# Two blocks of a transformer on one core: the moving columns of every gemm pass read as i and i+128 in turns

## The chip, the cores and the metric

The kernel runs on one core of one Trainium2 chip (trn2). The metric is device time in microseconds (us) of one execution; the median of the runs is compared. TensorE, VectorE (DVE in the profile), ScalarE (ACT), GpSimd (POOL) and SyncE (SP, which here issues the weight loads) run side by side and meet at semaphores.

## The reference

Two transformer blocks over one sequence of 256 tokens with 2048 channels, everything in float32. Cut to what matters here, it is a long row of products of a 256-row activation with a weight matrix:

```python
def first_block(x, ...):
    h = x + _gla_mixer(_rmsnorm(x, gla_norm), ...)       # h @ w_in (q, k, v, r), gated linear attention, @ w_out
    h = h + _sq_relu_mlp(_rmsnorm(h, mlp_norm), w_up, w_down)
    return _rmsnorm(h, final_norm)

def _sq_relu_mlp(h, w_up, w_down):                        # 2048 -> 8192 -> 2048
    a = jax.nn.relu(h @ w_up)
    return (a * a) @ w_down

def second_block(x, ...):
    proj = rms_norm(x, norm_mix_g) @ w_in                 # q, k, v, conv and gate inputs, three branch gates
    y_a, y_b, y_c = ...                                   # attention, gated recurrence, short convolution
    x = x + (g_a * y_a + g_b * y_b + g_c * y_c) @ w_out
    x = x + jnp.square(jax.nn.relu(rms_norm(x, norm_mlp_g) @ w_mlp_up)) @ w_mlp_down
    return rms_norm(x, final_g)
```

## The kernel before

**Arithmetic of a product.** TensorE multiplies in the format fp32r, which holds fewer bits than float32. So each operand is split into a high part (a copy cast to fp32r) and a low part (what the copy lost), and a product is the sum of high x high, high x low and low x high. Activations lie transposed in SBUF, channels on partitions: `xs`, `hs`, `mixs` and `ycs` are `[128, k-tile, 2, 256]`, where the 2 is high and low and the 256 are tokens. Weights are loaded in units of 4 k-tiles x 256 columns (512 KB) into one of four slots of `raw`; ScalarE writes the high part (L820) and VectorE the low part (L1142) into `wsp`.

**A pass.** `gemm` (L509) produces one block of 256 output channels by 256 tokens. It goes over its units (usually four, 16 k-tiles), and for each k-tile over the two halves `j` of 128 output channels. For each it issues a pair of matmuls into the PSUM tile `acc[:, g, j]`, two rows of 256 columns: L530 takes the high weights as stationary operand and streams 512 moving columns, the 256 high tokens and the 256 low tokens, so that row 0 gets high x high and row 1 high x low; L532 takes the low weights, streams the 256 high tokens and adds into row 1. Where the result is wanted with tokens on partitions (the blocks "gv" and "v", `tokens_out`), the roles change: L525 and L527 take a tile of the activation as stationary operand and stream the weights, which `both_parts` views as `[128, 2, 256]`. In all cases the moving columns are read in the order in which they lie, 256 neighbours and then 256 others.

```python
pe.matmul(acc[:, g, j], w_part(0, slot)[:, t, cols], x[:, k0 + k], start=start,
          stop=False, skip_group_check=True)
ins = pe.matmul(acc[:, g, j, 1], w_part(1, slot)[:, t, cols], x[:, k0 + k, 0],
                start=False, stop=stop, skip_group_check=True)
```

**After a pass.** `g` alternates, so the sums of one pass are read while the next runs; a pass begins when the sums of the pass two before it have been read (`main_read`). ScalarE copies row 1 of both halves into `corr` (`evac`, L831); VectorE adds row 0 and `corr` into `z` (`take`, L1152, and the same line in `first_take` for the first block). From `z` the rest follows: scaling, squared relu, residual, split into high and low for the next product. The last block of the kernel has a tail of its own, `finish` (L1394 on VectorE, L1009 on ScalarE), with the additions split by half (L1399, L1401, L1402, L1405).

**Order of the work.** Each engine has its program written out by hand; the same walk over the blocks (`straight_walk`, `mlp_walk`, `mix_walk`) is used on all of them. ScalarE and VectorE split the weights of the next block while TensorE runs this one. The attention, gating, recurrence and norm matmuls (L612, L643, L658, L761 and others) are plain fp32 or fp32r matmuls between passes, and a short extra matmul (`spacer`, L507) stands in some passes.

Of the kernel before, what the change touches and what calls it, by code (L numbers as in the profile page):

```python
# [16 lines left out]
ALU = mybir.AluOpType  # L17
# [3 lines left out]
P = 128  # L21
# [96 lines left out]
def build(nc, a, out, scratch):  # L118
# [3 lines left out]
    def at(name, shape, dt=F32, offset=None):  # L122
        size = -(-int(np.prod(shape[1:])) * 4 // 32) * 32
        if offset is None:
            offset = top[0]
            top[0] += size
        return nc.alloc_sbuf_tensor_at(name, shape, dt, offset=offset)
# [6 lines left out]
    def w_part(k, slot):  # L134

        n = UK * NB
        start = HIGHS + k * LOWS + slot * n
        return wsp[:, start:start + n].rearrange("p (t n) -> p t n", t=UK)

    def both_parts(slot, t):  # L140

        row = (slot * UK + t) * NB
        return wsp[:, HIGHS:HIGHS + 2 * LOWS].rearrange("p (k n) -> p k n", k=2)[:, :, row:row + NB]
# [41 lines left out]
    corr = at("corr", [P, 2, 2, T])  # L185
    z = at("z", [P, 2, T])
# [32 lines left out]
    def psum(name, shape):  # L219
        return ctx.enter_context(nc.psum_tensor(name, shape, F32))  # L220

    acc = psum("acc", [P, 2, 2, 2, T])
# [3 lines left out]
    def sem(name):  # L226
        return ctx.enter_context(nc.semaphore(name))
# [3 lines left out]
    corr_ready, main_read = sem("corr_ready"), sem("main_read")  # L231
# [32 lines left out]
    end_corr, end_main, end_sum, end_sq = sem("end_corr"), sem("end_main"), sem("end_sum"), sem("end_sq")  # L264
# [4 lines left out]
    def prm(name, j=0, n=1):  # L269
        r = ROWS[name][0] + j  # L270
        return par[:, bass.ds(r, n)] if not isinstance(r, int) else par[:, r:r + n]

    def bc(ap, n=2):

        return ap[:].unsqueeze(1).to_broadcast([P, n, T])

    def kt_of(t, k):

        return t[:, k] if isinstance(k, int) else t[:, bass.ds(k, 1)].squeeze(1)
# [53 lines left out]
    def units_of(round_, first, n):  # L333

        return [(round_ + (first + k) // SLOTS, (first + k) % SLOTS) for k in range(n)]
# [162 lines left out]
    def _(pe):  # L498
# [6 lines left out]
        def spacer(to):  # L505

            pe.matmul(to[:, 0:SPACE], xs[:, 0, 0, 0:P], xs[:, 0, 0, 0:SPACE], start=True, stop=True, skip_group_check=True)  # L507

        def gemm(b, units, g, x, ready, k0=0, tokens_out=False, mid=None, before=None, mid_unit=2, spaced=False):  # L509

            if not (isinstance(b, int) and b < 2):
                pe.wait_ge(main_read, b - 1)
            for u, (rnd, slot) in enumerate(units):
                if before:
                    before(u)
                pe.wait_ge(lo_done, SLOTS * rnd + slot + 1)
                for s, v in ready(u):
                    pe.wait_ge(s, v)
                for t in range(UK):
                    k = UK * u + t  # L520
                    start, stop = k == 0, (u == len(units) - 1 and t == UK - 1)
                    for j in range(2):
                        cols = slice(j * P, j * P + P)
                        if tokens_out:
                            pe.matmul(acc[:, g, j], x[:, k0 + k, 0, cols], both_parts(slot, t), start=start,  # L525
                                      stop=False, skip_group_check=True)
                            ins = pe.matmul(acc[:, g, j, 1], x[:, k0 + k, 1, cols], w_part(0, slot)[:, t],  # L527
                                            start=False, stop=stop, skip_group_check=True)
                        else:
                            pe.matmul(acc[:, g, j], w_part(0, slot)[:, t, cols], x[:, k0 + k], start=start,  # L530
                                      stop=False, skip_group_check=True)
                            ins = pe.matmul(acc[:, g, j, 1], w_part(1, slot)[:, t, cols], x[:, k0 + k, 0],  # L532
                                            start=False, stop=stop, skip_group_check=True)
                        if spaced is True and u == t == j == 0:
                            spacer(acc[:, g, 1, 0])
                        if spaced == "late" and u == 0 and (t, j) == (UK - 1, 0):
                            spacer(flat[1])
                        if mid and u == mid_unit + 1 and (t, j) == (UK - 1, 0):
                            spacer(flat[1])
                ins.then_inc(unit_used, 1)  # L540
                if mid and u == mid_unit:
                    mid()
# [243 lines left out]
        for k in range(3):  # L786
            if k:
                pe.wait_ge(end_sq, k)
            for j in range(TT):
                part = sq[:, 0, k - 1, j * P:(j + 1) * P] if k else ssq[:, 0, j * P:(j + 1) * P]  # L790
                ins = pe.matmul(flat[2 * j][:, 0:2], part, ones[:, 0:2], start=(k == 0), stop=(k == 2),
                                skip_group_check=True)
# [5 lines left out]
    def look_ahead(rnd, first, n):  # L798

        return units_of(rnd + 1, first, n)  # L800
# [6 lines left out]
    def _(act):  # L807
# [32 lines left out]
        def squares(n, i, gain=None):  # L840

            if not (n == 1 and isinstance(i, int) and i == 0):
                act.wait_ge(ssq_done, 8 * (n - 1) + i)
            ins = act.activation(sq[:, 0], pair(xres, i), ACT.Square)  # L844
            if gain:
                for j in range(2):
                    ins = act.activation(sq[:, 1, j], kt_of(xres, 2 * i + j), ACT.Square, scale=prm(gain, 2 * i + j))
            ins.then_inc(sq_ready, 1)
# [281 lines left out]
    def _(dve):  # L1130
        own = Steps(dve, dve_steps)
# [6 lines left out]
        def split_lo(rnd, slot):  # L1138
            if is_past_end(rnd):
                return  # L1140
            dve.wait_ge(hi_done, SLOTS * rnd + slot + 1)
            dve.tensor_tensor(w_part(1, slot), raw[:, slot], w_part(0, slot).bitcast(F32),  # L1142
                              ALU.subtract).then_inc(lo_done, 1)

        def take(b, rnd, first, n, g, then=None):

            for r, s in look_ahead(rnd, first, n)[:-1]:
                split_lo(r, s)
            if then:
                then()  # L1150
            dve.wait_ge(corr_ready, b + 1)
            dve.tensor_tensor(z[:], acc[:, g, :, 0], corr[:, g], ALU.add).then_inc(main_read, 1)  # L1152
            dve.wait_ge(main_read, b + 1)

        def last_split(rnd, first, n):
# [8 lines left out]
        def gained(i, gain):  # L1164

            for j in range(2):
                g = gmix[:, bass.ds(2 * i + j, 1)] if gain == "gmix" else prm(gain, 2 * i + j)
                ins = dve.tensor_scalar(h[:, j], kt_of(xres, 2 * i + j), g, None, ALU.mult)
            ins.then_inc(value_ready, 1)
# [9 lines left out]
        for i in range(PAIRS):  # L1179
            dve.wait_ge(hi_ready, i + 1)  # L1180
            for j in range(2):
                ins = dve.scalar_tensor_tensor(out=xs[:, 2 * i + j, 1], in0=M[i % 4][:, j], scalar=prm("gla_norm", 2 * i + j),
                                               in1=xs[:, 2 * i + j, 0].bitcast(F32), op0=ALU.mult, op1=ALU.subtract)
# [6 lines left out]
        def first_take(g):  # L1190

            for u in range(4):
                split_lo(1, u)
            dve.wait_ge(std_done, 1)
            own.done(dve.reciprocal(rcol[:], rcol[:]))
            dve.wait_ge(const_done, 1)
            for j in range(TT):
                ins = dve.tensor_scalar(h[:, 0, j * P:(j + 1) * P], ident[:], rcol[:, j:j + 1], None, ALU.mult)
            ins.then_inc(diag_ready, 1)
            dve.wait_ge(corr_ready, 1)  # L1200
            dve.tensor_tensor(z[:], acc[:, g, :, 0], corr[:, g], ALU.add).then_inc(main_read, 1)
            dve.wait_ge(main_read, 1)

        def first_keys():
# [189 lines left out]
        def finish(rnd, g, gain):  # L1394

            r, s = units_of(rnd, 0, 4)[-1]
            x = [kt_of(xres, 2 * (PAIRS - 1) + j) for j in range(2)]
            dve.wait_ge(unit_used, SLOTS * r + s + 1)
            dve.tensor_tensor(x[1], x[1], acc[:, g, 1, 0], ALU.add).then_inc(end_main, 1)  # L1399
            dve.wait_ge(end_corr, 1)  # L1400
            own.done(dve.tensor_tensor(x[0], x[0], acc[:, g, 0, 0], ALU.add))  # L1401
            dve.tensor_tensor(x[0], x[0], corr[:, g, 0], ALU.add).then_inc(end_sum, 1)  # L1402
            dve.wait_ge(end_main, 1)
            dve.wait_ge(end_corr, 2)
            dve.tensor_tensor(x[1], x[1], corr[:, g, 1], ALU.add).then_inc(end_sum, 1)  # L1405
            dve.wait_ge(end_sum, 2)
            dve.wait_ge(y_mm, PAIRS - 1)
            gained(PAIRS - 1, gain)
# [199 lines left out]
```

## Time and profile before

| | |
|---|---|
| runs (us) | 2659.05, 2659.95, 2656.82; median 2659.05 |
| profiled execution, span from first to last instruction | 2658.5 us; no separate time of this execution is given |
| TensorE matmul busy | 2642.8 us, 99% |
| weight loads into TensorE busy | 2336.9 us, 88% |
| VectorE, ScalarE, GpSimd busy | 1787.8 (67%), 1350.7 (51%), 96.3 us (4%) |
| chain that ended last | TensorE 94%, DMA 3%, VectorE 2%, ScalarE 1% |
| DMA | 504.65 MB, mean 190 GB/s |
| mean granted TensorE clock | 0.998 |

How to read it: a row of the profile names a line of the kernel, the engine, the operation, out<-in by the names of the tiles, shapes and a count. Matmuls are pipelined and each row's duration includes the way through the array, so the durations of neighbours overlap; the distance from one start to the next is what a matmul occupies. "Idle before" is the time that an engine stood still just before a group, with what ended it. The clock is given as a share of full speed, 2.4 GHz; the other level is 1.2 GHz.

### The profile page before, as it was taken

The page shows a single profiled execution, that of the slowest core. Times are in us where ns is not written, and L with a number is a line of the kernel's source. Part 1 is how long each engine was busy: PE and PEld are TensorE (multiplying, and loading weights), DVE is VectorE, ACT ScalarE, POOL GpSimd, SP SyncE. Part 2 cuts the span into 40 slices and gives each one's busy share as a digit, 9 for nine tenths or more (in the row PEclk, how much of TensorE's full clock was granted, in tenths as well). Part 3 has the DMA queues.
Part 4 walks back from the last instruction along what each step waited for, and adds up shares of the span by engine and source line. Part 5 has one row for each costly group of instructions (what it writes and reads, how often), then busy time and mean ns, then how long its engine had stood idle before and what let it go on. Part 6 is the DMA issues. An engine that isn't in the chain of part 4 may idle for free.

```text
span 2658.5 us, 43594 instructions
## 1 busy us (share of the span) xinstructions
PE 2642.8 (99%) x15628; PEld 2336.9 (88%) x15628; DVE 1787.8 (67%) x2067; ACT 1350.7 (51%) x1635; POOL 96.3 (4%) x96
## 2 busy tenths in 40 slices
PE   9999999999999999999999999999999999999998
PEld 8888888888888888888888888888888888888887
DVE  6667777666566567866887666666776566665665
ACT  6546555444444445544675555555554444444444
POOL 1000020000000002200000000000110000000001
PEclk9999999999999999999999999999999999999999
DMA  7794666666666666665556655566666666666664
GB/s 223 167 212 129 205 192 194 192 190 193 194 190 197 194 192 189 211 208 167 159 180 192 198 190 189 189 193 202 196 191 191 190 192 196 190 196 196 191 194 138
DMA packets 507428, 504.65 MB, mean 190 GB/s; under 512 B 17908, under 2 KB 505609, under 8 KB 507337
## 3 DMA queue, kind: packets, MB, share of 16 engines
q1 hardware_dynamic: 506060, 501.79, 60.5%
q10 hardware_dynamic: 1276, 1.63, 1.5%
q8 instruction: 59, 0.97, 0.2%
q14 instruction: 33, 0.26, 0.0%
HBM read 499.69 MB, written 3.67 MB: 189 GB/s over the span
## 4 chain that ended last, share of the span: by engine, by line
PE 94%; DMA 3%; DVE 2%; ACT 1%; issue 0%; SPq 0%; DVEq 0%; ACTq 0%
PE acc L530 60%; PE acc L532 30%; DMA raw<-in_gla_w_in 3%; PE acc L525 1%; DVE wsp L1142 1%; PE acc L527 1%; ACT wsp L820 0%; DVE lat L1474 0%; DMA xtok<-in_x 0%; PE misc L643 0%; PE misc L658 0%; PE misc L761 0%; PE misc L612 0%; PE misc L660 0%; PE misc L581 0%
## 5 line engine op out<-in xcount | busy, mean ns | idle before, releaser
L1142 DVE TENSOR_TENSOR wsp<-raw,wsp 128x1024 fp32r<-128x1024 f32 x944 | 1166.6, 1242 | 577.4 <-ACT wsp L820 547.1
L530 PE MATMUL acc<-xs,wsp 128*128 128x512 f32 x4224 | 1446.8, 390 | 1.1 <-issue 0.4
L820 ACT ACTIVATE wsp<-raw 128x1024 fp32r<-128x1024 f32 x944 | 993.4, 1057 | 688.1 <-PE acc L532 602.0
L532 PE MATMUL acc<-xs,wsp 128*128 128x256 f32 x4224 | 1166.5, 276 | 0.0
L530 PEld LDWEIGHTS acc<-xs,wsp 128*128 128x128 f32 x4224 | 793.4, 188 | 166.3 <-DVE wsp L1142 1.8
L530 PE MATMUL acc<-hs,wsp 128*128 128x512 f32 x2560 | 873.0, 389 | 0.0
L532 PEld LDWEIGHTS acc<-xs,wsp 128*128 128x128 f32 x4224 | 793.4, 188 | 0.5
L532 PE MATMUL acc<-hs,wsp 128*128 128x256 f32 x2560 | 706.6, 276 | 0.0
L530 PEld LDWEIGHTS acc<-hs,wsp 128*128 128x128 f32 x2560 | 480.6, 188 | 99.4
L532 PEld LDWEIGHTS acc<-hs,wsp 128*128 128x128 f32 x2560 | 480.6, 188 | 0.0
L831 ACT ACTIVATE corr<-acc 128x512 f32<-128x512 f32 x246 | 146.9, 597 | 370.1 <-PE acc L532 360.1
L1152 DVE TENSOR_TENSOR z<-acc,corr 128x512 f32<-128x512 f32 x246 | 169.9, 691 | 215.3 <-ACT corr L831 215.2
L525 PE MATMUL acc<-wsp,xs 128*128 128x512 f32 x384 | 134.9, 395 | 1.7 <-issue 1.7
L471 POOL TENSOR_TENSOR ssq<-ssq,sq 128x256 f32<-128x256 f32 x37 | 30.4, 828 | 2495.7 <-ACT sq L844 1842.8
L527 PE MATMUL acc<-wsp,xs 128*128 128x256 f32 x384 | 107.1, 279 | 0.0
L525 PEld LDWEIGHTS acc<-wsp,xs 128*128 128x128 f32 x384 | 72.1, 188 | 19.7 <-issue 2.7
L530 PE MATMUL acc<-mixs,wsp 128*128 128x512 f32 x256 | 87.1, 389 | 0.0
L838 ACT ACTIVATE hs<-z 128x512 f32 (+1 forms) x64 | 40.5, 633 | 90.6 <-DVE z L1370 90.6
L527 PEld LDWEIGHTS acc<-wsp,xs 128*128 128x128 f32 x384 | 72.0, 188 | 0.0
L532 PE MATMUL acc<-mixs,wsp 128*128 128x256 f32 x256 | 70.7, 276 | 0.0
L1349 DVE TENSOR_TENSOR xres<-xres,z 128x512 f32 (+1 forms) x79 | 54.7, 693 | 12.1 <-DVE z L1152 11.8
L530 PEld LDWEIGHTS acc<-mixs,wsp 128*128 128x128 f32 x256 | 48.1, 188 | 9.8
(243 smaller groups left out, 1059.8 us busy)
## 6 DMA issues: line engine op xcount, KB each, us to landing
raw<-in_w_in SPq DMA_DIRECT2D x224, 512.0 KB, 4.4
raw<-in_mlp_w_up SPq DMA_DIRECT2D x128, 512.0 KB, 4.0
raw<-in_mlp_w_down SPq DMA_DIRECT2D x128, 512.0 KB, 4.4
raw<-in_w_mlp_up SPq DMA_DIRECT2D x128, 512.0 KB, 4.0
raw<-in_w_mlp_down SPq DMA_DIRECT2D x128, 512.0 KB, 4.2
raw<-in_gla_w_in SPq DMA_DIRECT2D x96, 512.0 KB, 4.9
raw<-in_gla_w_out SPq DMA_DIRECT2D x32, 512.0 KB, 4.2
raw<-in_w_out SPq DMA_DIRECT2D x32, 512.0 KB, 4.0
```

The costliest lines, as they stand in the source:

```text
L471: pool.tensor_tensor(ssq[:, k], ssq[:, k], sq[:, k, 0], ALU.add).then_inc(ssq_half, 1)
L525: pe.matmul(acc[:, g, j], x[:, k0 + k, 0, cols], both_parts(slot, t), start=start, stop=False, skip_group_check=True)
L527: ins = pe.matmul(acc[:, g, j, 1], x[:, k0 + k, 1, cols], w_part(0, slot)[:, t], start=False, stop=stop, skip_group_check=True)
L530: pe.matmul(acc[:, g, j], w_part(0, slot)[:, t, cols], x[:, k0 + k], start=start, stop=False, skip_group_check=True)
L532: ins = pe.matmul(acc[:, g, j, 1], w_part(1, slot)[:, t, cols], x[:, k0 + k, 0], start=False, stop=stop, skip_group_check=True)
L820: act.activation(w_part(0, slot), raw[:, slot], ACT.Copy).then_inc(hi_done, 1)
L831: act.activation(corr[:, g], acc[:, g, :, 1], ACT.Copy).then_inc(corr_ready, 1)
L838: act.activation(pair(dst, i)[:, :, 0], src[:], ACT.Copy).then_inc(hi_ready, 1)
L1142: dve.tensor_tensor(w_part(1, slot), raw[:, slot], w_part(0, slot).bitcast(F32), ALU.subtract).then_inc(lo_done, 1)
L1152: dve.tensor_tensor(z[:], acc[:, g, :, 0], corr[:, g], ALU.add).then_inc(main_read, 1)
L1349: own.done(dve.tensor_tensor(pair(xres, i), pair(xres, i), z[:], ALU.add))
```

## The change

All matmuls of `gemm` read their moving operand through a view, `taking_turns`, that takes column i and column i+128 of each 256 in turns: 0, 128, 1, 129, and so on. High and low parts stay apart, so a 512-column matmul reads the 256 high ones in this order and then the 256 low ones. They write the PSUM columns in the order in which they come, one next to the other, so that PSUM column 2i holds column i and 2i+1 holds i+128. ScalarE's copy to `corr` keeps that order. The additions that join the two sums read PSUM and `corr` through `in_order`, every second column and then the ones between, and write their result in natural order, seen as two halves (`halves`). The stationary operands, the matmuls outside `gemm`, the semaphores and the number of instructions of each engine stay as they are.

```diff
+    def taking_turns(ap):
+
+        dims = "p s (u i) -> p s i u" if len(ap.shape) == 3 else "p (u i) -> p i u"
+        return ap.rearrange(dims, u=2)
+
+    def in_order(ap):
+
+        dims = "p s (i u) -> p s u i" if len(ap.shape) == 3 else "p (i u) -> p u i"
+        return ap.rearrange(dims, u=2)
+
+    def halves(ap):
+
+        dims = "p s (u i) -> p s u i" if len(ap.shape) == 3 else "p (u i) -> p u i"
+        return ap.rearrange(dims, u=2)
...
                     for j in range(2):
-                        cols = slice(j * P, j * P + P)
+                        cols, both = slice(j * P, j * P + P), acc[:, g, j].rearrange("p a b -> p (a b)")
                         if tokens_out:
-                            pe.matmul(acc[:, g, j], x[:, k0 + k, 0, cols], both_parts(slot, t), start=start,
+                            pe.matmul(both, x[:, k0 + k, 0, cols], taking_turns(both_parts(slot, t)), start=start,
                                       stop=False, skip_group_check=True)
-                            ins = pe.matmul(acc[:, g, j, 1], x[:, k0 + k, 1, cols], w_part(0, slot)[:, t],
+                            ins = pe.matmul(acc[:, g, j, 1], x[:, k0 + k, 1, cols], taking_turns(w_part(0, slot)[:, t]),
                                             start=False, stop=stop, skip_group_check=True)
                         else:
-                            pe.matmul(acc[:, g, j], w_part(0, slot)[:, t, cols], x[:, k0 + k], start=start,
+                            pe.matmul(both, w_part(0, slot)[:, t, cols], taking_turns(x[:, k0 + k]), start=start,
                                       stop=False, skip_group_check=True)
-                            ins = pe.matmul(acc[:, g, j, 1], w_part(1, slot)[:, t, cols], x[:, k0 + k, 0],
+                            ins = pe.matmul(acc[:, g, j, 1], w_part(1, slot)[:, t, cols], taking_turns(x[:, k0 + k, 0]),
                                             start=False, stop=stop, skip_group_check=True)
...
-            dve.tensor_tensor(z[:], acc[:, g, :, 0], corr[:, g], ALU.add).then_inc(main_read, 1)
+            dve.tensor_tensor(halves(z[:]), in_order(acc[:, g, :, 0]), in_order(corr[:, g]), ALU.add).then_inc(main_read, 1)
...
+            x = [halves(xj) for xj in x]
-            dve.tensor_tensor(x[1], x[1], acc[:, g, 1, 0], ALU.add).then_inc(end_main, 1)
+            dve.tensor_tensor(x[1], x[1], in_order(acc[:, g, 1, 0]), ALU.add).then_inc(end_main, 1)
             dve.wait_ge(end_corr, 1)
-            own.done(dve.tensor_tensor(x[0], x[0], acc[:, g, 0, 0], ALU.add))
-            dve.tensor_tensor(x[0], x[0], corr[:, g, 0], ALU.add).then_inc(end_sum, 1)
+            own.done(dve.tensor_tensor(x[0], x[0], in_order(acc[:, g, 0, 0]), ALU.add))
+            dve.tensor_tensor(x[0], x[0], in_order(corr[:, g, 0]), ALU.add).then_inc(end_sum, 1)
             dve.wait_ge(end_main, 1)
             dve.wait_ge(end_corr, 2)
-            dve.tensor_tensor(x[1], x[1], corr[:, g, 1], ALU.add).then_inc(end_sum, 1)
+            dve.tensor_tensor(x[1], x[1], in_order(corr[:, g, 1]), ALU.add).then_inc(end_sum, 1)
```

## Rows read from the trace of the kernel before

**Rows 1.** The page: span, busy times and the granted clock in 40 slices.
```profile
span 2658.5 us, 43594 instructions
...
PE 2642.8 (99%) x15628; PEld 2336.9 (88%) x15628; DVE 1787.8 (67%) x2067; ACT 1350.7 (51%) x1635; POOL 96.3 (4%) x96
...
PEclk9999999999999999999999999999999999999999
```

**Rows 2.** The page: the chain that ended last, by engine and line.
```profile
PE 94%; DMA 3%; DVE 2%; ACT 1%; issue 0%; SPq 0%; DVEq 0%; ACTq 0%
PE acc L530 60%; PE acc L532 30%; DMA raw<-in_gla_w_in 3%; PE acc L525 1%; DVE wsp L1142 1%; PE acc L527 1%; ACT wsp L820 0%; DVE lat L1474 0%; DMA xtok<-in_x 0%; PE misc L643 0%; PE misc L658 0%; PE misc L761 0%; PE misc L612 0%; PE misc L660 0%; PE misc L581 0%
```

**Rows 3.** Groups by line: shapes, count, busy us, mean ns, idle before.
```profile
L530 PE MATMUL acc<-xs,wsp 128*128 128x512 f32 x4224 | 1446.8, 390 | 1.1 <-issue 0.4 <-DVE wsp L1142 0.4
...
L532 PE MATMUL acc<-xs,wsp 128*128 128x256 f32 x4224 | 1166.5, 276 | 0.0
...
L530 PE MATMUL acc<-hs,wsp 128*128 128x512 f32 x2560 | 873.0, 389 | 0.0
...
L525 PE MATMUL acc<-wsp,xs 128*128 128x512 f32 x384 | 134.9, 395 | 1.7 <-issue 1.7
...
L530 PE MATMUL acc<-mixs,wsp 128*128 128x512 f32 x256 | 87.1, 389 | 0.0
...
L530 PE MATMUL acc<-ycs,wsp 128*128 128x512 f32 x128 | 43.9, 389 | 0.0
```

**Rows 4.** Busy time by stretch, 500 us of the first MLP.
```profile
core 0: us, PE busy (x) PEld busy (x) DVE busy (x) ACT busy (x) POOL busy (x), PEclk, DMA share, GB/s
500.00:1000.00 500.00, 500.00 (x2943) 442.88 (x2942) 315.67 (x322) 229.46 (x253) 0.00 (x0) 1.00 0.62 193
```

**Rows 5.** TensorE in order of time (start us, us), in both MLPs.
```profile
600.00 0.39 PE L530 MATMUL acc<-xs,wsp 128*128 128x512 f32 x1
600.22 0.28 PE L532 MATMUL acc<-xs,wsp 128*128 128x256 f32 x1
600.34 0.39 PE L530 MATMUL acc<-xs,wsp 128*128 128x512 f32 x1
...
2640.07 0.39 PE L530 MATMUL acc<-hs,wsp 128*128 128x512 f32 x1
2640.30 0.28 PE L532 MATMUL acc<-hs,wsp 128*128 128x256 f32 x1
2640.41 0.39 PE L530 MATMUL acc<-hs,wsp 128*128 128x512 f32 x1
```

**Rows 6.** The same view in the two token-major stretches.
```profile
135.09 0.39 PE L525 MATMUL acc<-wsp,xs 128*128 128x512 f32 x1
135.32 0.28 PE L527 MATMUL acc<-wsp,xs 128*128 128x256 f32 x1
135.43 0.39 PE L525 MATMUL acc<-wsp,xs 128*128 128x512 f32 x1
...
1199.80 0.40 PE L525 MATMUL acc<-wsp,xs 128*128 128x512 f32 x1
1200.04 0.28 PE L527 MATMUL acc<-wsp,xs 128*128 128x256 f32 x1
1200.16 0.40 PE L525 MATMUL acc<-wsp,xs 128*128 128x512 f32 x1
```

**Rows 7.** Plain fp32 matmuls, 256 columns: order of time, and their group.
```profile
1290.46 1.03 PE L761 MATMUL misc<-lat,wax 128*128 128x256 f32 x4
...
L761 PE MATMUL misc<-lat,wax 128*128 128x256 f32 x32 | 8.2, 379 | 0.0
```

**Rows 8.** Groups by line on VectorE: far steps against neighbours.
```profile
L1283 DVE TENSOR_TENSOR btot<-btot,mn 128x8 f32<-128x8 f32 x3 | 0.5, 173 | 0.1
L1285 DVE TENSOR_TENSOR dec<-btot 128x8 f32<-128x8 f32 x6 | 0.6, 163 | 0.0
...
L1142 DVE TENSOR_TENSOR wsp<-raw,wsp 128x1024 fp32r<-128x1024 f32 x944 | 1166.6, 1242 | 577.4 <-ACT wsp L820 547.1 <-DVE hs L1160 17.0 <-DVE mixs L1160 0.4
L1349 DVE TENSOR_TENSOR xres<-xres,z 128x512 f32 (+1 forms) x79 | 54.7, 693 | 12.1 <-DVE z L1152 11.8
```

**Rows 9.** The joining additions: their group, and order of time at the end.
```profile
L1152 DVE TENSOR_TENSOR z<-acc,corr 128x512 f32<-128x512 f32 x246 | 169.9, 691 | 215.3 <-ACT corr L831 215.2
...
2647.83 0.42 DVE L1401 TENSOR_TENSOR xres<-xres,acc 128x256 f32<-128x256 f32 x1
...
2648.28 0.42 DVE L1402 TENSOR_TENSOR xres<-xres,corr 128x256 f32<-128x256 f32 x1
2648.63 0.42 DVE L1405 TENSOR_TENSOR xres<-xres,corr 128x256 f32<-128x256 f32 x1
```

**Rows 10.** Waits: who waited for whom, us in total, times, longest.
```profile
ACT wsp L820 <- PE acc L532: 602.0, 442, 1.7
DVE wsp L1142 <- ACT wsp L820: 547.1, 501, 6.2
ACT corr L831 <- PE acc L532: 360.1, 223, 2.2
DVE z L1152 <- ACT corr L831: 215.2, 220, 1.5
```

More of the change, by code:

```diff
@@ L1200, in first_take @@
             dve.wait_ge(corr_ready, 1)
-            dve.tensor_tensor(z[:], acc[:, g, :, 0], corr[:, g], ALU.add).then_inc(main_read, 1)
+            dve.tensor_tensor(halves(z[:]), in_order(acc[:, g, :, 0]), in_order(corr[:, g]), ALU.add).then_inc(main_read, 1)
             dve.wait_ge(main_read, 1)
```

## The prediction

> **What bounds the kernel now.** I read the page's busy shares first: TensorE works 99% of a span of 2658.5 us, and its granted clock is at the upper level in every slice [rows 1]. The chain that ended last gives TensorE 94%, of which 90% are the two matmuls of a gemm pass, L530 and L532 [rows 2]. Then the count: 4224 + 2560 + 256 + 128 = 7168 pairs of a 512-column and a 256-column matmul there, and 384 such pairs in the two token-major groups, L525 and L527, 7552 pairs in all [rows 3]. Busy time says little about matmuls that overlap, so I take the distance between starts. In the MLP stage 2943 matmuls fill 500 us, 0.340 us a pair, with the clock at 1.00 [rows 4]; single starts there alternate by 0.23 and 0.11 us [rows 5]. Token-major pairs follow at 0.34 us at 135 us and at 0.35 to 0.36 us at 1200 us [rows 6]; I take 0.350.
>
> So the gemms hold 7168 x 0.340 + 384 x 0.350 = 2571.5 us, and everything else 2658.5 - 2571.5 = 87.0 us (the start, the attention and norm matmuls between passes, the end). This is the span of the profiled execution, for which no time of its own is given besides; it lies 0.55 us under the median of the three runs, 2659.05, so no correction is made.
>
> The cadence holds a second reading. 768 columns at 2.4 GHz are 0.320 us; the pair takes 0.340, that is 1.0625 times as long, or 17 cycles for 16 columns. Plain fp32 matmuls of 256 columns don't show this: four of them run 1.03 us from the first start to the last end, one lasts 0.379, so starts lie (1.03 - 0.379) / 3 = 0.217 us apart [rows 7], which is two cycles per column (0.2133) and 3.4 ns. So where a column is wanted only every second cycle nothing is lost, and where it is wanted every cycle a sixteenth is added. I read that as the moving operand's supply being already at its limit when its columns lie next to each other.
>
> **What the change removes, adds and moves.** No instruction is added or removed on any engine; shapes and semaphores stay. Three access patterns differ.
>
> First, the moving operand of all 2 x 7552 gemm matmuls. The next column read now lies 128 floats, 512 bytes, away, then one float after the first, and so on; no two columns read in succession are neighbours. No matmul of the trace reads like this, so its price is bounded. From below: nothing, or even a gain, if the supply can follow two streams: the sixteenth may go, and a pair take half of three plain fp32 matmuls, 0.5 x 3 x 0.217 = 0.3255 us. From above: VectorE shows what far steps cost a reading engine. The additions at L1283, which read 8 elements 1 KB apart, take 173 ns, those at L1285, all neighbours, 163: (173 - 163) / 8 = 1.25 ns more for each element. Its contiguous price is (1242 - 693) / 512 = 1.07 ns, from the 1024- and 512-element rows [rows 8]. So a far step about doubles an element there. If TensorE paid the same 1.25 ns on top of its 0.340 / 768 = 0.443 ns for each column, a pair would take 768 x 1.69 = 1.30 us.
>
> Between these I take the doubling, not the 1.25 ns: the nearest row is the fp32 matmul, the one in which TensorE gets one four-byte column in two cycles and the supply keeps up without loss. A pair is then 768 x 2 / 2.4 = 640 ns, and 3.4 ns for each of its two matmuls, 0.6468 us. 7552 x 0.6468 = 4885 us.
>
> The Trainium skill, "Advanced Engine Details and Errata", section "SBUF Cachelines", speaks against this change: an SBUF line has 16 bytes, two hits on a line are needed to cover its access latency, and a new line at each access is penalised. No row here shows it for TensorE, and it gives no size; by it the sum would rise by an amount it leaves open. The same skill's "TensorE: Matmul & The Clock Gate", section "Step-by-step: what each phase is for", says that one moving column enters per cycle whatever it is; the trace at 17 cycles for 16 columns disagrees already. By that rule a pair would cost its 0.320 us before and after.
>
> Second, the order of PSUM. The matmuls still write neighbouring PSUM columns: nothing. The copy of the correction half is unchanged. The addition that joins the sums (L1152, 246 times, 691 ns) now reads PSUM and corr two floats apart. Bounds: nothing, since a step of 8 bytes is short, and a doubled element, 512 x 1.07 = 0.55 us a time, 135 us in all [rows 9]. I take nothing for the end time either way. A sum must be read before the pass after next starts, one whole pass of 32 pairs or 10.9 us later, and VectorE is busy 1788 of 2658 us and waits mostly for others [rows 1, 10]. If that cover were gone, 135 us would be the price.
>
> Third, the end: three of the additions of 256 elements at L1401, L1402 and L1405 lie one after the other behind the last matmul [rows 9]. Doubled, they add 3 x 256 x 1.07 = 0.8 us; I take nothing.
>
> With the matmuls at 0.6468 us a pair all other engines have more room. The 87.0 us beside the gemms may lose a few us where a pass waits for weights now; I leave them. Sum: 4885 + 87 = 4972 us, say 4970.
>
> **The likeliest case's own range.** Lower end: two cycles a column and nothing per matmul, 7552 x 0.640 + 87 = 4920, less some 10 us for waits that the slower matmuls swallow. Upper end: today's pair doubled whole, sixteenth included, 0.680 and 0.700 us: 7168 x 0.680 + 384 x 0.700 + 87 = 5230.
>
> **Rivals.**
> *Two streams are supplied as well as one, and better.* If the lost cycle in 17 comes from one stream running from one stretch of SBUF into the next, reading two in turns could hide it. For it: the plain fp32 matmuls show that the array itself can do without that cycle [rows 7]. Against it: every column now makes such a jump, where one in sixteen did. The pair becomes 0.3255 us, the time 7552 x 0.3255 + 87 = 2545 us, faster by 4.3%. It decides as soon as the cadence falls under 0.340. Chance 0.14.
> *Nothing changes.* The supply may hold the last piece read of each stream, so that both run at the present 17 for 16: 2659 us, with the doubled additions hidden. Also here if the pattern is split into other instructions without cost. For it: the cadence is the same 0.34 for moving tiles xs and hs at quite different places of SBUF [rows 5], so it doesn't hang on where the columns lie. Against: nothing shows a second piece being kept. Chance 0.07.
> *A part is paid.* One column of each pair of turns finds its piece and the other pays a cycle: 1.5 cycles a column, 0.480 us a pair, 7552 x 0.480 + 87 = 3712 us; for it, only that it lies between the ends. Chance 0.11.
> *More than double.* The 1.25 ns per far step of VectorE is paid by TensorE too: 7552 x 1.30 + 87 = 9905 us. For it the additions at L1283, against it that on VectorE the far step doubled a price rather than showed a fixed latency. Chance 0.06.
> That leaves 0.62 for the doubling.
>
> **How the numbers follow.** The forecast is the likeliest case, 4970. The range goes from 2650 to 5240: it holds the doubling (0.62), the part paid (0.11) and no change (0.07), 0.80 together, and leaves out the gain and the more than double. Within the doubling alone it would be 4910 to 5230. What a measurement can tell from no change is some 0.2%, 5 us. Faster 0.14, within it 0.07, slower 0.79 (0.62 + 0.11 + 0.06).
>
> **What would show it.** Right: starts of the 512-column matmul 0.43 us before the 256-column one and that 0.217 before the next; TensorE still busy 99% at a clock of 1.00; some 1540 matmuls in 500 us of the MLP stage instead of 2943; VectorE's busy time in us nearly the same and its share near 36%; DMA down to some 100 GB/s. The addition at L1152 between 0.69 and 1.24 us, without anyone on TensorE waiting for it. Wrong: a cadence of 0.34 or less, or of 0.5 or over 0.7 us a pair; matmuls that wait for VectorE between passes; or a clock at the lower level for long stretches, which would double today's cadence with no fault of the supply.

## The result, and the profile after

The changed kernel takes 2568.64 us (median of 4 runs, 2567.33 to 2570.86) against 2658.41 before: ratio 0.966, 95% interval 0.965 to 0.968. It is 90 us faster where 4970 us were forecast, and outside the range. In the profiled execution the span fell from 2658.5 to 2566.6 us, by 91.9.

The page of the changed kernel, its span, busy times, clock and chain by engine, for [rows 1, 2]:

```profile
span 2566.6 us, 43594 instructions
...
PE 2546.3 (99%) x15628; PEld 2336.8 (91%) x15628; DVE 1815.6 (71%) x2067; ACT 1348.3 (53%) x1635; POOL 95.8 (4%) x96
...
PEclk9999999999999999999999999999999999999999
...
PE 94%; DMA 3%; DVE 2%; ACT 1%; issue 0%; SPq 0%; DVEq 0%; ACTq 0%
```

Nothing has changed places: TensorE still sets the end. Busy time by stretch, the first MLP, for [rows 4]:

```profile
500.00:1000.00 500.00, 500.00 (x3056) 459.73 (x3055) 337.34 (x340) 241.72 (x271) 4.78 (x5) 1.00 0.64 200
```

3056 matmuls stand where 2943 stood: 500 / 1528 = 0.327 us a pair after 0.340. TensorE in order of time (start us, us) in the same stretch, and then in the token-major one, for [rows 5, 6]:

```profile
599.74 0.38 PE L545 MATMUL acc<-xs,wsp 128*128 128x512 f32 x1
599.96 0.27 PE L547 MATMUL acc<-xs,wsp 128*128 128x256 f32 x1
600.07 0.38 PE L545 MATMUL acc<-xs,wsp 128*128 128x512 f32 x1
...
124.34 0.38 PE L540 MATMUL acc<-wsp,xs 128*128 128x512 f32 x1
124.56 0.27 PE L542 MATMUL acc<-wsp,xs 128*128 128x256 f32 x1
124.67 0.38 PE L540 MATMUL acc<-wsp,xs 128*128 128x512 f32 x1
```

Both are 0.33 now, and the 0.34 and 0.35 that the token-major pairs had are one cadence. The sum: 7168 x (0.340 - 0.3272) = 91.8 us and 384 x (0.350 - 0.3272) = 8.8 us, 100.5 in all, of which 91.9 arrived.

Part of the difference is a stage in which TensorE isn't the bound. The chain of waits there, in order of time (start us, us), before and after:

```profile
111.23 1.07 ACT wsp L820
112.29 0.02 issue
112.32 1.24 DVE wsp L1142
113.56 0.02 issue
113.57 9.17 DMA raw<-in_gla_w_in
...
135.82 1.07 ACT wsp L820
```
```profile
107.87 1.07 ACT wsp L835
108.94 0.02 issue
108.97 1.24 DVE wsp L1157
110.20 0.02 issue
110.22 9.11 DMA raw<-in_gla_w_in
...
132.28 1.07 ACT wsp L835
```

Two blocks of this chain (load, ScalarE's split, VectorE's split, the slot free for the next load) take 135.82 - 111.23 = 24.6 us before and 132.28 - 107.87 = 24.4 after. Faster matmuls don't shorten it, they reach its end sooner and wait. The changed kernel's TensorE rows (start us, us) and the busy times by stretch at that place:

```profile
119.33 0.62 PE L540 MATMUL acc<-wsp,xs 128*128 128x512 f32 x1 [3.07 <-issue]
119.74 0.42 PE L542 MATMUL acc<-wsp,xs 128*128 128x256 f32 x1
119.95 0.64 PE L540 MATMUL acc<-wsp,xs 128*128 128x512 f32 x1
120.38 0.42 PE L542 MATMUL acc<-wsp,xs 128*128 128x256 f32 x1
120.59 0.63 PE L540 MATMUL acc<-wsp,xs 128*128 128x512 f32 x1
```
```profile
118.00:120.00 2.00, 0.67 (x3) 0.62 (x4) 2.00 (x2) 1.56 (x2) 0.00 (x0) 0.87 0.89 316
120.00:122.00 2.00, 2.00 (x8) 1.73 (x8) 1.92 (x3) 1.97 (x5) 0.00 (x0) 0.50 0.83 228
```

TensorE stands still for 3.07 us, and after it the granted clock is at the lower level, 1.2 GHz (0.50), where a pair takes 0.64 us instead of 0.327. Five pairs at the lower clock took 5 x (0.64 - 0.327) = 1.6 us more. Over the whole run TensorE's idle time, span less busy time, is 2566.6 - 2546.3 = 20.3 us where it was 2658.5 - 2642.8 = 15.7, so 4.6 us of the gain went into waiting. Two groups of the changed kernel, for [rows 3], hold nearly all of it:

```profile
L545 PE MATMUL acc<-xs,wsp 128*128 128x512 f32 x4224 | 1394.0, 383 | 3.5 <-DVE wsp L1157 3.0 <-issue 0.2
...
L540 PE MATMUL acc<-wsp,xs 128*128 128x512 f32 x384 | 128.1, 386 | 3.8 <-issue 3.8
```

The idle time before the 512-column matmuls that stream `xs` is 3.5 us, 3.0 of it for VectorE's weights, where it was 1.1; before the token-major ones it is 3.8 where it was 1.7. That leaves 100.5 - 91.9 - 1.6 - 4.6 = 2.4 us, which lie within the rounding of the cadences.

The joining addition did get dearer, for [rows 9], and the additions at the end didn't:

```profile
L1167 DVE TENSOR_TENSOR z<-acc,corr 128x512 f32<-128x512 f32 x246 | 200.2, 814 | 184.6 <-ACT corr L846 184.5
...
2555.91 0.42 DVE L1417 TENSOR_TENSOR xres<-xres,acc 128x256 f32<-128x256 f32 x1
2556.37 0.43 DVE L1418 TENSOR_TENSOR xres<-xres,corr 128x256 f32<-128x256 f32 x1
2556.71 0.42 DVE L1421 TENSOR_TENSOR xres<-xres,corr 128x256 f32<-128x256 f32 x1
```

691 ns became 814, 246 x 0.123 = 30 us of VectorE's time, which cost the span nothing that a row shows: TensorE never waits for this addition. The additions of 256 elements at the end take 0.42 to 0.43 us each, as before. They aren't the same form at half the size: only one of their two inputs is read with a step, `acc` or `corr`, and the other, `xres`, lies contiguous.

### The profile page after: what moved, and what is told of

Read it like the earlier page. It is cut to its first block, busy times and chain, and to the rows that moved or that the text cites. A ratio compares the mean times of both kernels' runs of the same rounds, so it can differ in the third digit from the quotient of the medians.

```text
span 2566.6 us, 43594 instructions
## 1 busy us (share of the span) xinstructions
PE 2546.3 (99%) x15628; PEld 2336.8 (91%) x15628; DVE 1815.6 (71%) x2067; ACT 1348.3 (53%) x1635; POOL 95.8 (4%) x96
## 4 chain that ended last, share of the span: by engine, by line
PE 94%; DMA 3%; DVE 2%; ACT 1%; issue 0%; SPq 0%; DVEq 0%; ACTq 0%
PE acc L545 60%; PE acc L547 30%; DMA raw<-in_gla_w_in 3%; PE acc L540 2%; DVE wsp L1157 1%; PE acc L542 1%; DVE lat L1490 0%; ACT wsp L835 0%; DMA xtok<-in_x 0%; PE misc L658 0%; PE misc L673 0%; PE misc L776 0%; PE misc L627 0%; PE misc L675 0%; DVE lat L1486 0%
## 5 line engine op out<-in xcount | busy, mean ns | idle before, releaser
L545 PE MATMUL acc<-xs,wsp 128*128 128x512 f32 x4224 | 1394.0, 383 | 3.5 <-DVE wsp L1157 3.0
L547 PE MATMUL acc<-xs,wsp 128*128 128x256 f32 x4224 | 1151.5, 273 | 0.0
L545 PEld LDWEIGHTS acc<-xs,wsp 128*128 128x128 f32 x4224 | 798.7, 189 | 116.7 <-DVE wsp L1157 5.0
L545 PE MATMUL acc<-hs,wsp 128*128 128x512 f32 x2560 | 841.0, 382 | 0.0
L547 PEld LDWEIGHTS acc<-xs,wsp 128*128 128x128 f32 x4224 | 811.2, 192 | 0.4
L547 PE MATMUL acc<-hs,wsp 128*128 128x256 f32 x2560 | 697.8, 273 | 0.0
L545 PEld LDWEIGHTS acc<-hs,wsp 128*128 128x128 f32 x2560 | 483.9, 189 | 67.2
L547 PEld LDWEIGHTS acc<-hs,wsp 128*128 128x128 f32 x2560 | 491.5, 192 | 0.0
L1167 DVE TENSOR_TENSOR z<-acc,corr 128x512 f32<-128x512 f32 x246 | 200.2, 814 | 184.6 <-ACT corr L846 184.5
L540 PE MATMUL acc<-wsp,xs 128*128 128x512 f32 x384 | 128.1, 386 | 3.8 <-issue 3.8
L486 POOL TENSOR_TENSOR ssq<-ssq,sq 128x256 f32<-128x256 f32 x37 | 30.1, 823 | 2407.4 <-ACT sq L859 1778.8
L489 POOL TENSOR_TENSOR ssq<-ssq,sq 128x256 f32<-128x256 f32 x37 | 55.9, 1519 | 2.3
```

Source lines behind the costliest of these rows:

```text
L486: pool.tensor_tensor(ssq[:, k], ssq[:, k], sq[:, k, 0], ALU.add).then_inc(ssq_half, 1)
L489: ins = pool.tensor_tensor(ssq[:, k], ssq[:, k], sq[:, k, 1], ALU.add)
L540: pe.matmul(both, x[:, k0 + k, 0, cols], taking_turns(both_parts(slot, t)), start=start, stop=False, skip_group_check=True)
L545: pe.matmul(both, w_part(0, slot)[:, t, cols], taking_turns(x[:, k0 + k]), start=start, stop=False, skip_group_check=True)
L1167: dve.tensor_tensor(halves(z[:]), in_order(acc[:, g, :, 0]), in_order(corr[:, g]), ALU.add).then_inc(main_read, 1)
```

## The experiments

Each kernel below changes nothing but the order in which the moving columns are read and written back, unless told otherwise. The diffs are cut, and stand against the changed kernel unless told otherwise. Each kernel was run once, where no number of runs is given; of the kernel before and the changed one, repeated runs lie within 5 us of each other. What I compare is the number of pairs in the stretch from 500 to 1000 us. For the kernel before and those near it this lies in the first MLP; in the kernels with a step the first 200 us or so of it are still gemm passes ahead of the MLP.

### One stream with a step

The two kernels read even columns and then odd ones, or every 16th column. Both replace the views. The additions read PSUM and `corr` as they lie and write their result with the step:

```diff
-        dims = "p s (u i) -> p s i u" ...      # taking_turns, u=2
+        dims = "p s (i u) -> p s u i" ...      # u=2 (step of 2) or u=16 (step of 16)
-        dims = "p s (i u) -> p s u i" ...      # in_order
+        dims = "p s (u i) -> p s u i" ...      # natural
```

Step of 2 columns:

> Every gemm pass reads one stream with a step: all even columns, then all odd ones (step 8 bytes), and the joining addition writes its result back in natural order. Today's spans: 2658.5 us with neighbours in succession (0.340 us a pair), 2566.6 with i and i+128 in turns (0.3275 a pair; 93 us lie beside the 7552 pairs). Theory N (neighbours): what costs the cycle in 17 is that each column read is the neighbour of the one before, so any order without that is free: 0.3275 a pair, about 2567 us. Theory J (jumps): a stream that leaves a 64-byte stretch pays a cycle, and two streams in turns hide it; here one stream leaves a stretch every 8 columns, 768/8 = 96 cycles = 0.040 us, so 0.360 a pair and 7552 x 0.360 + 93 = 2812 us.

Step of 16 columns:

> One stream again, with a step of 16 columns (64 bytes): 0, 16, 32 ... then 1, 17, 33 and so on. Theory N: free, 0.3275 a pair, about 2567 us. Theory J: every column leaves its stretch and there is no second stream to hide it, at least two cycles a column, 0.640 a pair, 7552 x 0.640 + 93 = 4926 us.

Measured: 5240.3 us and 5019.2 us, beside 2659.0 for the kernel before. Busy times in the stretch, step 2 and then step 16:

```profile
500.00:1000.00 500.00, 500.00 (x1470) 305.09 (x1470) 173.28 (x195) 129.42 (x149) 14.08 (x17) 1.00 0.31 96
```
```profile
500.00:1000.00 500.00, 500.00 (x1533) 315.46 (x1532) 185.80 (x197) 131.79 (x151) 13.95 (x17) 1.00 0.32 100
```

0.680 us and 0.652 us a pair, 2.13 and 2.04 cycles a column at 2.4 GHz. Theory N, that only neighbours in succession cost, has fallen with both. Theory J, jumps out of a 64-byte stretch, has the size of step 16 about right (0.640 us a pair) and that of step 2 (0.360) wrong by nearly a factor of two: a step of 8 bytes within one stream costs twice the time, and 0.680 is exactly twice 0.340, the extra cycle in 17 included. So my forecast's price exists. It is that of one stream with a step, not that of two streams in turns.

### How far apart the two streams must lie

Here column i and column i + d take turns within blocks of 2d columns. The 512 moving columns are one run for this, token-major pairs read in natural order, and the addition is made for each half of the channels by itself. It reads PSUM and `corr` as they lie and writes `z` in turns.

```diff
-        dims = "p s (u i) -> p s i u" ...      # u=2
+        dims = "p s (b u i) -> p s b i u" ...  # u=2, i=d, with d = 2, 4, 8, 16
+            for j in range(2):
+                ins = dve.tensor_tensor(halves(z[:, j]), in_order(acc[:, g, j, 0]), in_order(corr[:, g, j]), ALU.add)
```

> Columns i and i+16 in turns within each 32 (64 bytes apart), in the 7168 pairs with channels on the output's partitions; the 384 token-major pairs read in natural order, and the joining addition is made in two halves. Theory N: 0.3275 a pair, 0.350 in the token-major ones, 2567 + 384 x 0.0225 = 2576 us. Theory J: two streams that take turns, each leaving its stretch as in the changed kernel: the same 2576. A theory of banks (B), by which 512 bytes between the two streams matter and 64 don't give another bank: 0.340, 2658 us.

> Columns i and i+2 in turns within each 4, so 0, 2, 1, 3, 4, 6, 5, 7: the reads jump about by 8 bytes but walk through each 64-byte stretch once, as the natural order does; token-major pairs in natural order. Theory N: 3 of 4 columns are no neighbour of the one before (2 to 1 and 3 to 4 are next to it, one of these forwards): 0.3275 to 0.331 a pair, 2576 to 2600 us. Theory J: one stream through each stretch once, nothing changed, 0.340, 2658 us.

> Columns i and i+8 in turns within each 16: two streams 32 bytes apart that stay in the same 64-byte stretch, otherwise as with i and i+16 (2573.2 us of span) and i and i+2 (2657.0). If the stretch that matters is 64 bytes long, whether crossing it costs (theory J) or staying in it does (theory S), nothing is gained: 0.340 a pair, 2657 us. If any distance over 8 or 16 bytes does, 0.3275 and 2573 us. A stretch of 32 bytes would give 2573 as well.

> Columns i and i+4 in turns within each 8, two streams 16 bytes apart; otherwise as with i+8 (2573.1 us of span) and i+2 (2657.0). Theory L (two readers that serve the odd and the even positions of the stream, each with a 16-byte line of its own: a line that serves 4 reads of its reader costs nothing, 2 reads a cycle in 17, 1 read about double): each reader gets four columns out of a line, 0.3275 a pair, 2573 us. Theory A (what costs is going on to the adjoining line, as the natural order does every 4 columns): the two streams are adjoining lines and so is the next, 0.340, 2657 us.

Measured (all beside 2659.0 to 2659.8 for the kernel before):

| order | us | matmuls in 500 us | us a pair |
|---|---|---|---|
| i, i+2 | 2658.8 | 2943 | 0.340 |
| i, i+4 | 2572.3 | 3055 | 0.327 |
| i, i+8 | 2574.9 | 3056 | 0.327 |
| i, i+16 | 2574.9 | 3056 | 0.327 |
| i, i+128 (the change) | 2568.6 | 3056 | 0.327 |

The rows for i+2 and for i+4:

```profile
500.00:1000.00 500.00, 500.00 (x2943) 442.69 (x2942) 319.76 (x368) 229.47 (x254) 0.00 (x0) 1.00 0.62 193
```
```profile
500.00:1000.00 500.00, 500.00 (x3055) 459.89 (x3054) 348.63 (x388) 240.27 (x271) 4.96 (x5) 1.00 0.64 200
```

The step lies between 8 and 16 bytes of distance, sharply, and above it, up to 512 bytes, no distance matters. The kernels with i+2 and i+4 differ in one number; the matmuls, their shapes and the order of PSUM are the same. The addition writes `z` in another order, and it got dearer with i+4 (640 ns after 420 for 256 elements), so it isn't what gains. It is the order of reading the moving columns. That ends theory J, which wanted i and i+8, inside one 64-byte stretch, at 0.340. It ends theory A as well, the cost of going on to the adjoining 16 bytes, which wanted i and i+4 at 0.340. The order i, i+2 goes through 16-byte pieces one after the other as the natural order does, and costs the same; with i+4 two such pieces are open and each serves four reads. The 4 to 6 us by which these three lie above the changed kernel fit the token-major pairs, left in natural order: 9 us by the expectation, less the 1.6 us of the pairs at the lower clock, which their traces don't have at that place, and some 1 us of waiting (idle 18.7 to 19.6 us where the changed kernel has 20.3).

### Runs in turns, and four streams

To separate "two streams" from "each piece used by every second read", the 256-column matmuls of the kernel before were made to read runs from the two halves in turns. Nothing puts their sums in order, so the product low x high lands on other tokens. The diff stands against the kernel before.

```diff
+    def in_runs(ap):
+
+        return ap.rearrange("p (u b i) -> p b u i", u=2, i=8)      # or i=2
...
-                            ins = pe.matmul(acc[:, g, j, 1], w_part(1, slot)[:, t, cols], x[:, k0 + k, 0],
+                            ins = pe.matmul(acc[:, g, j, 1], w_part(1, slot)[:, t, cols], in_runs(x[:, k0 + k, 0]),
```

> The kernel before, but the 256-column matmuls with channels on the output's partitions (7168 of them) read runs of 8 neighbouring columns from the two halves in turns: 0 to 7, 128 to 135, 8 to 15 ... Their sums are not put back in order, so the product low x high lands on other tokens. A 256-column matmul takes 113.3 ns in natural order and 109 in turns. Each 64-byte stretch is now entered twice, 32 entries instead of 16. Theory J (entering a stretch costs a cycle unless the two streams alternate word by word): 106.7 + 32 / 2.4 = 120 ns, 2658.5 + 7168 x 0.0067 = 2706 us. Theory S (what costs is a stay of 16 columns in one stretch; reads that leave it after 8 give it time): 109 ns, 2658.5 - 7168 x 0.0043 = 2628 us.

> The same with runs of 2 columns: 0, 1, 128, 129, 2, 3 ... (products of low x high again on other tokens). Each run is one 8-byte word and the next word lies in the other half, so words alternate as in the changed kernel, but each is read once. Theory J and theory S both: 109 ns, 2628 us. If instead the gain of the changed kernel needs each word to be used twice with another between (a word kept), or columns that are no neighbours in succession, it stays at 113.3 or lies in between: 2644 to 2658 us.

Measured: 2738.1 us with runs of 8 and 3107.2 with runs of 2. Busy times by stretch, runs of 8 and then runs of 2:

```profile
500.00:1000.00 500.00, 500.00 (x2859) 440.76 (x2859) 304.78 (x308) 221.17 (x244) 0.00 (x0) 1.00 0.60 188
```
```profile
500.00:1000.00 500.00, 500.00 (x2481) 446.20 (x2480) 267.95 (x273) 193.82 (x215) 0.00 (x0) 1.00 0.52 163
```

A pair takes 0.350 and 0.403 us. Less the 0.227 of a 512-column matmul in natural order, the 256 columns take 0.123 and 0.176 us, against 0.113 in natural order and 0.109 in turns. Theory S, that leaving a stretch early gives it time, falls at once. Theory J's 120 ns and 2706 us are in the right direction for runs of 8 and far off for runs of 2, for which J and S had 109 and the third reading 113.3 at most. Two streams by themselves are not what helps: of the three lengths of run, going over after each second column costs most, after every single column it costs nothing.

That left theory L, two readers that serve the odd and the even positions of the stream and hold a 16-byte piece each. In turns, with at least 16 bytes between, each reader stays in one piece for four reads. In natural order, with i+2, and with runs of 8, it gets two reads out of a piece; with a step of 2 or 16, or runs of 2, it changes at every read. The runs of 8 speak against L already: by it their 256 columns would take the 0.113 us of the natural order, and they took 0.123. The last test takes four streams:

```diff
-        return ap.rearrange(dims, u=2)
+        return ap.rearrange(dims, u=4)
```

> Four streams in turns in all 7552 pairs: columns i, i+64, i+128, i+192, the addition puts them back. Each 16-byte line still serves four columns within 16 positions, but a reader of every second position changes its line at each read. Theory L: one read per line and reader, about double, 0.52 (as runs of 2, at 1.6 cycles a column) to 0.68 us a pair (as step 8 bytes), 7552 x 0.52 + 93 = 4020 to 5230 us. A theory of any few lines held at a time (W), for which the two streams of the changed kernel are nothing special: 0.3275, 2567 us.

Measured: 3315.5 us, from this stretch:

```profile
500.00:1000.00 500.00, 500.00 (x2345) 393.01 (x2344) 271.33 (x263) 183.57 (x205) 0.00 (x0) 1.00 0.50 155
```

0.4264 us a pair, 1.33 cycles a column. This is neither theory's number. The theory of any few pieces held (W) is out, since four streams cost 30% where two cost nothing. L has the direction and not the size: a reader that changes its piece at each read, but comes back to it in the read after, pays less than one that doesn't. L sorts the orders roughly: four reads a piece 1.02 cycles a column, two 1.06 (but 1.15 in runs of 8), one with a return 1.33 and 1.65, one without 2.04 and 2.13. It gives neither the numbers nor the difference between the natural order and runs of 8, so it is a picture that fits in part and not a cause that is shown.

**At the lower clock.** Shortly after the start, TensorE's clock is at the lower level in some of these runs, and the same orders can be read there. The kernel before, in natural order, and then the kernel with four streams (start us, us; and the granted clock of the stretch):

```profile
13.11 0.41 PE L532 MATMUL acc<-xs,wsp 128*128 128x256 f32 x1
13.32 0.63 PE L530 MATMUL acc<-xs,wsp 128*128 128x512 f32 x1
13.75 0.38 PE L532 MATMUL acc<-xs,wsp 128*128 128x256 f32 x1
12.50:13.70 1.20, 1.20 (x5) 1.06 (x4) 1.20 (x3) 1.20 (x4) 0.00 (x0) 0.50 1.09 387
```
```profile
13.69 0.63 PE L545 MATMUL acc<-xs,wsp 128*128 128x512 f32 x1
14.11 0.41 PE L547 MATMUL acc<-xs,wsp 128*128 128x256 f32 x1
14.32 0.63 PE L545 MATMUL acc<-xs,wsp 128*128 128x512 f32 x1
13.10:15.10 2.00, 2.00 (x8) 1.70 (x8) 2.00 (x6) 1.75 (x4) 0.00 (x0) 0.50 1.20 254
```

In natural order 256 columns take 0.21 us and 512 take 0.43, 0.64 a pair, and four streams take 0.64 as well (14.32 - 13.69 = 0.63). That is 768 cycles of 1.2 GHz: one order loses no seventeenth there, the other no third. The kernel with a step of 2 takes 0.69 us a pair there, nearly the 0.680 of the upper clock:

```profile
13.58 0.63 PE L544 MATMUL acc<-xs,wsp 128*128 128x512 f32 x1
...
16.33 0.63 PE L544 MATMUL acc<-xs,wsp 128*128 128x512 f32 x1
13.00:16.50 3.50, 3.50 (x12) 2.78 (x11) 3.50 (x8) 2.71 (x6) 0.00 (x0) 0.50 0.97 202
```

Four pairs lie between these starts, (16.33 - 13.58) / 4 = 0.69. So an order seems to have a price in time that doesn't follow TensorE's clock (0.340 us a pair in natural order, 0.426 for four streams, 0.68 for a step of 2), and the longer one of this price and the 768 cycles counts. These are few matmuls, two of them in natural order, but they speak for the supply of the columns as the place of the loss, and against the array.

### Repeat, and a version without spacers

The spacers are short extra matmuls that stand in chosen passes. The expectations count 33 of them; the page of the kernel before has 15628 matmuls and that of the kernel without them 15591, so there are 37, and 37 x 0.09 = 3.3 us. The token-major passes of the kernel before run at two cadences, 0.344 and 0.353 us a pair, and passes with a spacer are among both; in turns all run at 0.3275. The kernel without spacers tests whether they are of any use now.

```diff
-            pe.matmul(to[:, 0:SPACE], xs[:, 0, 0, 0:P], xs[:, 0, 0, 0:SPACE], start=True, stop=True, skip_group_check=True)
+            return
```

> The changed kernel without the 33 extra matmuls of 200 columns. [...] If reading in turns leaves only one cadence, as all token-major pairs of the changed kernel at 0.3275 suggest, they are of no use now and each returns its 0.09 us: 2566.6 - 33 x 0.09 = 2563.6 us of span. [...]

> The changed kernel again, beside the kernel before and beside the changed kernel without spacers: 2568.6 us, ratio 0.966.

> The changed kernel without the 33 spacers, timed: one look gave 2565.2 us, 3.4 us under the changed kernel's median. If that is real, 33 x 0.09 = 3 us, the median lies at 2565 to 2566 and the ratio to the kernel before near 0.965; if the look was chance, it is the same as the changed kernel, 2568.6.

A first single run gave 2565.2 us. Timed on one chip, in five runs each and nine of the kernel before (median 2659.75): the changed kernel 2568.22 us (2566.09 to 2568.94), ratio 0.9656, interval 0.9643 to 0.967; without spacers 2564.24 us (2563.18 to 2566.00), ratio 0.9643, interval 0.963 to 0.9657. The intervals against the kernel before overlap, but the two sets of five runs don't: the slowest without spacers lies below the fastest with them. The difference of the medians is 4.0 us, against 3.3 us worked out. In the MLP stretch the cadence is that of the changed kernel:

```profile
500.00:1000.00 500.00, 500.00 (x3055) 459.89 (x3054) 335.53 (x341) 242.30 (x271) 6.52 (x7) 1.00 0.64 200
```

This is the fastest version of the study. Whether the spacers did anything for the kernel before, and what sets its two cadences, no run tests.

## Why the prediction was wrong

**What held.** The frame did: TensorE's cadence sets the span, the gemms are 2 x 7552 matmuls, and the reading of the cadence as 17 cycles for 16 columns, with no such loss where a column is wanted every second cycle [rows 7], is what the change removed. The plain fp32r matmuls outside the gemms, left in natural order, are a control within the changed kernel itself, in order of time:

```profile
37.63 1.53 PE L627 MATMUL misc<-xs,wgs 128*128 128x512 f32 x6
```

Six of 512 columns, each 0.39 us long, so (1.53 - 0.39) / 5 = 0.228 us from start to start, the 0.227 of the natural order. In the same execution the 256-column matmuls in turns start 0.218 us after the 512-column ones. The kernels with i+2 and i+4 say the same of the gemms themselves. And the reading that the supply of the moving operand is at its limit is supported by the rows at the lower clock, where the natural order loses nothing.

**The step that failed** is the price of the moving operand: "Between these I take the doubling". Three things went into it. Its size, two cycles a column, was that of the plain fp32 matmul [rows 7], and nothing tied that to columns in turns. I took "no two columns read in succession are neighbours" for the property that costs, and it isn't: with i and i+128 in turns none are neighbours and the cost is lower than with all neighbours. And the evidence from VectorE [rows 8] was one stream with a far step, which is nearer to what the kernels with a step of 2 and of 16 columns read. These took 5240 and 5019 us; the range given for the doubling was 4910 to 5230, so the forecast was about right for another kernel. In its place the runs showed that columns in turns cost 0.327 us a pair, 1.02 cycles a column and not two.

**The rival that came true** is the first, two streams supplied as well as one and better: 0.3255 us a pair and 2545 us worked out, 0.327 and 2568.6 measured. It had 0.14. Its mechanism, a stream that runs from one stretch of SBUF into the next, is not borne out for the stretch that it had in mind, 16 columns or 64 bytes (i and i+8 gain everything within one such stretch). For a stretch of 16 bytes the table neither shows nor excludes it. I had set against it that every column now makes a jump where one in sixteen did, and this is the same mistake again, a price put on each jump without regard to the order around it. That the time went down is thus the rival's number come true, with its reason open. Its 2545 us are worked out from the span, which came out as 2566.6: 22 us more, of which the cadence is 7552 x 0.0017 = 13, and 6 the added waits and the pairs at the lower clock described above. The prediction had said that the 87.0 us beside the gemms would shrink or stay; that was for slower matmuls. With faster ones the parts that wait for weights grew.

**The Trainium skill** on SBUF lines ("Advanced Engine Details and Errata", section "SBUF Cachelines") was put down as speaking against this change. The order in turns gives each access another line and costs nothing, against it as the sentence stands; the step of 2 columns gives two consecutive hits on each 16-byte line, which it calls enough, and doubles the time. Its two numbers, 16 bytes and two hits, do turn up: the step between i+2 and i+4 is at 16 bytes of distance. The measurement decides on the rule as worded.

**Smaller terms.** "I take nothing for the end time either way" for the joining addition held: 814 ns, between the bounds of 691 and 1240, and hidden. "Doubled, they add 0.8 us" for the tail: nothing was added. That PSUM is written in the order of reading was priced at nothing, and the runs give no reason against it. The shuffle could also be undone by writing the PSUM columns straight to their final places; that wasn't tried.

## What to carry to other kernels

Where fp32r matmuls of 256 columns and more follow each other 6% later than one column a cycle, and the clock is at its upper level, let the moving operand take turns, column by column, between two places at least 16 bytes apart (16 to 512 were tried), and undo the shuffle in an instruction that reads the sums anyway and has cover. Don't read with a step instead: one stream with a step of 8 bytes doubled the time. And before a price for a new access pattern is taken from another engine's row, check that the row has the same pattern, here two streams and not one with a step.

## What the runs showed of the hardware that I had not expected

- Order of the moving columns, in cycles a column at 2.4 GHz, from pairs of 768 columns: 1.02 in turns at 16 bytes or more apart, 1.06 in natural order and with i, i+2, 1.33 for four streams, 2.04 and 2.13 for one stream with steps of 64 and of 8 bytes. In turns by runs, for the 256 columns alone: 1.15 in runs of 8 (0.123 us) and 1.65 in runs of 2 (0.176 us).
- At the lower clock the order costs little or nothing: pairs follow after 0.64 us, 768 cycles of 1.2 GHz, in turns (120.59 - 119.95), in natural order and with four streams, and after 0.69 us with a step of 2. The price of an order seems to be a time and not a number of TensorE's cycles.
- VectorE's addition with its two inputs read at a step of 8 bytes takes 814 ns for 512 elements, 123 more than contiguous. With one input at that step and the other contiguous, 256 elements in the tail take 0.42 us, as before.
- Why the natural order loses one cycle in 17, and the number for four streams, stay open.
